# Running the combining product of an expert pair inside the next pair, in five PSUM banks

## What is computed

```python
for e in range(N_EXPERTS):
    gu = t @ w_gate_up[e] + b_gate_up[e]
    gate = jnp.minimum(gu[:, :D_EXPERT], SWIGLU_LIMIT)
    up = jnp.clip(gu[:, D_EXPERT:], -SWIGLU_LIMIT, SWIGLU_LIMIT)
    h = (up + 1.0) * (gate * jax.nn.sigmoid(SWIGLU_ALPHA * gate))
    out = out + comb[:, e:e + 1] * (h @ w_down[e] + b_down[e])
```

## Time and profile before

| | |
|---|---|
| median of three runs | 1267.7 us |
| the profiled execution | 1268.49 us |
| its span from first to last instruction | 1266.7 us (1.8 us lie around it) |
| TensorE busy | 1208.8 us, 95% |
| VectorE, ScalarE, GpSimd busy | 28%, 18%, 2% |
| moved by DMA | 446.69 MB, mean 353 GB/s |
| mean granted TensorE clock | 0.998 |

### The profile page before, as it was taken

How to read it: one execution, slowest core, us unless ns; L and a number is a source line. 1 busy time by engine, 2 the same in 40 slices (tenths; PEclk the granted TensorE clock), 3 DMA queues, 4 the chain that set the end, 5 groups by cost and what they waited for, 6 DMA issues and landing times.

```text
span 1266.7 us, 14158 instructions
## 1 busy us (share of the span) xinstructions
PE 1208.8 (95%) x5416; PEld 525.9 (42%) x5416; DVE 360.7 (28%) x826; ACT 225.2 (18%) x406; POOL 28.2 (2%) x62
## 2 busy tenths in 40 slices
PE   5999999999999999999999999999999999999997
PEld 3777777543333333333333333333333333333342
DVE  3564001253223132313233132323131321313233
ACT  2575110043101011101101010111011010101024
POOL 1001004000000000000000000000000000000000
PEclk9999999999999999999999999999999999999999
DMA  9725533437999999999999999999999999999931
GB/s 304 286 87 211 191 121 129 138 150 299 427 430 429 429 426 429 429 428 427 428 429 428 428 428 429 428 429 427 430 429 428 426 429 429 428 427 428 429 155 37
DMA packets 51027, 446.69 MB, mean 353 GB/s; under 512 B 8070, under 2 KB 9190, under 8 KB 26328
## 3 DMA queue, kind: packets, MB, share of 16 engines
q1 hardware_dynamic: 48304, 440.30, 83.5%
q0 software_dynamic: 2592, 6.10, 1.7%
q10 hardware_dynamic: 112, 0.03, 0.0%
HBM read 444.90 MB, written 1.88 MB: 353 GB/s over the span
## 4 chain that ended last, share of the span: by engine, by line
PE 74%; DMA 14%; DVE 6%; ACT 3%; issue 3%; ACTq 0%; POOL 0%; DVEq 0%; SPq 0%; POOLq 0%
PE ps L837 27%; PE ps L622 17%; PE ps L854 14%; DMA ring<-in_w_gate_up 12%; PE ps L905 6%; PE ps L811 3%; PE ps L935 2%; PE ps L823 2%; PE ps L614 1%; DVE work L1514 1%; DVE work L1507 1%; DVE work L1511 1%; ACT work L1134 1%; DMA work<-in_b_down 1%; ACT poolw L1144 1%
## 5 line engine op out<-in xcount | busy, mean ns | idle before, releaser
L837 PE MATMUL ps<-ring,work 128*64 128x512 f32 x2048 | 446.4, 592 | 5.1 <-DMA ring<-in_w_gate_up 5.1
L837 PEld LDWEIGHTS ps<-ring,work 128*64 128x64 f32 x2048 | 144.7, 137 | 288.5 <-issue 269.8
L854 PE MATMUL ps<-ring,gate_a 128*64 128x512 f32 x1024 | 225.9, 594 | 0.0
L622 PE MATMUL ps<-work,ring 128*128 128x288 f32 x768 | 191.4, 411 | 0.8 <-DVE work L1213 0.7
L622 PEld LDWEIGHTS ps<-work,ring 128*128 128x128 f32 x768 | 147.4, 192 | 42.1 <-issue 1.0
L854 PEld LDWEIGHTS ps<-ring,gate_a 128*64 128x64 f32 x1024 | 71.2, 137 | 133.2 <-issue 128.7
L1507 DVE TENSOR_SCALAR work<-ps 128x512 f32<-128x512 f32 x32 | 22.1, 692 | 354.8 <-PE ps L837 354.8
L1526 DVE TENSOR_TENSOR u_tok<-u_tok,ps 128x512 f32<-128x512 f32 (+1 forms) x96 | 65.7, 684 | 166.7 <-PE ps L905 166.2
L1134 ACT ACTIVATE work<-work 128x512 f32<-128x512 f32 x32 | 20.2, 630 | 489.2 <-DVE work L1507 489.2
L905 PE MATMUL ps<-poolw 128*128 128x512 f32 (+1 forms) x192 | 79.0, 611 | 23.3 <-ACT poolw L1144 23.1
L803 PE MATMUL ps<-x_tok,work 128*64 128x512 f32 x396 | 90.6, 592 | 0.0
(11 more groups left out here) (217 smaller groups left out, 652.1 us busy)
## 6 DMA issues: line engine op xcount, KB each, us to landing
ring<-in_w_gate_up SPq DMA_DIRECT2D x128, 2048.0 KB, 19.3
ring<-in_w_down SPq DMA_DIRECT2D x64, 2048.0 KB, 19.6
ring<-in_w_in SPq DMA_DIRECT2D x8, 2048.0 KB, 13.5
ring<-in_w_proj_b SPq DMA_DIRECT2D x2, 2048.0 KB, 7.8
ring<-in_w_proj_a SPq DMA_DIRECT2D x2, 2048.0 KB, 10.6
ring<-in_w_out SPq DMA_DIRECT2D x2, 2048.0 KB, 7.6
ring<-in_w_ple_gate SPq DMA_DIRECT2D x4, 1024.0 KB, 21.8
x_tok<-in_x_prompt SPq DMA_DIRECT2D x2, 512.0 KB, 3.9
```

Source lines behind the costliest of these rows:

```text
L622: mm = pe.matmul(out(b), lhs, rhs, start=(k == 0), stop=(k == len(pairs) - 1))
L837: mm = pe.matmul(ps[half(g), b, :], xg[:, k, :], whole_piece(q)[:, at + 512 * g:at + 512 * g + 512], start=False, stop=(k == KC - 1))
L854: mm = pe.matmul(ps[half(g), b, :], hT[:, 4 * j + i, :], whole_piece(q)[:, at + 512 * g:at + 512 * g + 512], start=False, stop=(4 * j + i ...
```

## The change

The product of a pair (the new add_pair on TensorE) is no longer issued at the end of its pair. It is issued in the next pair, behind the gate/up product of that pair's first expert and ahead of its gather. Its six results go to five banks (4, 5, 6, 7, 3): each of the first four has one of its own, and the two halves of the 32-token tile share bank 3, in which the transposes of sel_w also land. VectorE adds the six results behind the activation of the same expert. The first pair of the loop issues the product too; for that, VectorE zeroes o_pair (128 x 1024) and sel_wT (128 x 384) behind the normalised embedding, and TensorE waits for both ahead of its loop. After the loop one more product is issued for the last pair: 17 in all where there were 16. The waits of the tail follow the new count.

```diff
@@ -70,7 +70,7 @@
 
 
 CHUNK_BANK = {"gate": 0, "hT": 0, "xT": 1, "up": 1, "x": 2, "out": 2}
-B_S, B_Y = 3, [4, 5, 6]
+B_S, B_Y = 3, [4, 5, 6, 7, 3]
 PAIRS = NE // 2
 
 GATE_LOADS, SMALL_LOADS = 4, 3
@@ -336,6 +336,7 @@
         x_cleared = sem("x_cleared")
         x1_copied = sem("x1_copied")
         sel_w_ready = sem("sel_w_ready")
+        pair_cleared = sem("pair_cleared")
         x2_squared = sem("x2_squared")
         t_filled = [sem(f"tail_filled{b}") for b in range(8)]
         t_emptied = [sem(f"tail_emptied{b}") for b in range(8)]
@@ -403,9 +404,13 @@
             bank, turn = chunk_turn(kind, n)
             eng.wait_ge(emptied[bank], turn + (bank_uses[bank] + 1))
 
-        def pair_bank(i):
-
-            return B_Y[i % 3], i // 3
+        def pair_bank(t, h):
+
+            return B_Y[2 * t + h] if t < TT - 1 else B_Y[-1]
+
+        def sums_before(bank, m):
+
+            return (m * 2 if bank == B_S else m) + bank_uses[bank]
 
         tail_turns = plan_tail()
 
@@ -858,6 +863,18 @@
                         mm.then_inc(piece_used_up[q], 1)
                 mm.then_inc(filled[b], 1)
 
+            def add_pair(m):
+
+                chunk_read(pe, "out", m * 2 - 1)
+                for t in range(TT):
+                    for h in range(2):
+                        bank = pair_bank(t, h)
+                        pe.wait_ge(emptied[bank], sums_before(bank, m))
+                        mm = pe.matmul(ps[column_half(("y", t, h)), bank, :], sel_wT[:, t, 0:ROWS[t]],
+                                       o_pair[:, 512 * h:512 * h + 512], start=True, stop=True)
+                        if t < TT - 1 or h == 1:
+                            mm.then_inc(filled[bank], 1)
+
             embed(2, [0, 1])
             embed(1, [0])
             gather(0)
@@ -865,6 +882,7 @@
             chunk_read(pe, "x", 0)
             turn_rows("xT", 0, x_blocks)
             pe.wait_ge(bias_cast, BIAS_PARTS)
+            pe.wait_ge(pair_cleared, 2)
             pe.wait_ge(passes_ready, 1)
             passes = pe.value_load(passes_i[0:1, 0:1], min_val=1, max_val=PASSES)
             with pe.Fori(0, passes) as c:
@@ -878,6 +896,8 @@
                         chunk_read(pe, "xT", n)
                         weigh_gate_up(n)
 
+                        if i == 0:
+                            add_pair(m)
                         gather(n + 1)
                         pe.wait_ge(hidden_ready, n + 1)
                         turn_rows("hT", n, h_blocks)
@@ -885,7 +905,7 @@
                         turn_rows("xT", n + 1, x_blocks)
                         if i == 1:
                             pe.wait_ge(sel_w_ready, m + 1)
-                            pe.wait_ge(emptied[B_S], m + bank_uses[B_S])
+                            pe.wait_ge(emptied[B_S], m * 2 + (bank_uses[B_S] + 1))
                             for t in range(TT):
                                 mm = pe.transpose(ps[:, B_S, t * P:t * P + P], sel_w[:, t, :], ident[:])
                             mm.then_inc(filled[B_S], 1)
@@ -894,16 +914,7 @@
                         chunk_read(pe, "hT", n)
                         weigh_down(n)
 
-                    pe.wait_ge(emptied[B_S], m + (bank_uses[B_S] + 1))
-                    chunk_read(pe, "out", n)
-                    for t in range(TT):
-                        for h in range(2):
-                            bank, turn = pair_bank(2 * t + h)
-                            pe.wait_ge(emptied[bank], m * 2 + (bank_uses[bank] + turn))
-                        for h in range(2):
-                            bank, turn = pair_bank(2 * t + h)
-                            pe.matmul(ps[column_half(("y", t, h)), bank, :], sel_wT[:, t, 0:ROWS[t]],
-                                      o_pair[:, 512 * h:512 * h + 512], start=True, stop=True).then_inc(filled[bank], 1)
+            add_pair(passes * PAIRS)
 
 
             def begin_tail(name):
@@ -913,7 +924,7 @@
                 return bank
 
             for bank in B_Y:
-                pe.wait_ge(emptied[bank], passes * NE + bank_uses[bank])
+                pe.wait_ge(emptied[bank], sums_before(bank, passes * PAIRS) + 1)
             for t in range(TT):
                 for h in range(2):
                     b = begin_tail(("x2T", t, h))
@@ -1134,7 +1145,7 @@
                         nc.scalar.activation(sg, gate, ACT.Sigmoid, scale=ALPHA).then_inc(sig_ready, 1)
                         copy_inputs(n + 1)
                         if i == 1:
-                            act.wait_ge(filled[B_S], m + (bank_uses[B_S] + 1))
+                            act.wait_ge(filled[B_S], m * 2 + (bank_uses[B_S] + 2))
                             nc.scalar.copy(sel_wT.rearrange("p t s -> p (t s)"), ps[:, B_S, 0:TT * P]) \
                                 .then_inc(emptied[B_S], 1)
 
@@ -1145,10 +1156,9 @@
 
 
             for t in range(TT):
-                for i in range(2 * TT):
-                    if i // 2 == t:
-                        bank, turn = pair_bank(i)
-                        act.wait_ge(emptied[bank], passes * NE + (bank_uses[bank] + turn - 1))
+                for h in range(2):
+                    bank = pair_bank(t, h)
+                    act.wait_ge(emptied[bank], sums_before(bank, passes * PAIRS) + 1)
                 if t:
                     act.wait_ge(squares[3], t)
                 square_sums(3, t, x2[0:ROWS[t], t, :], square_tail)
@@ -1465,6 +1475,17 @@
                 b = chunk_filled(dve, "xT", n)
                 V.tensor_tensor(in_halves(xg), by_channel(b), in_halves(xg_gain), ALU.mult).then_inc(emptied[b], 1)
 
+            def add_pair(m):
+
+                for t in range(TT):
+                    for h in range(2):
+                        bank = pair_bank(t, h)
+                        dve.wait_ge(filled[bank], sums_before(bank, m) + 1)
+                        x_half = x2[0:ROWS[t], t, 512 * h:512 * h + 512]
+                        ins = V.tensor_tensor(x_half, x_half, ps[column_half(("y", t, h)), bank, :], ALU.add)
+                        if t < TT - 1 or h == 1:
+                            ins.then_inc(emptied[bank], 1)
+
             dve.wait_ge(gain_landed, 16)
             gathered(0)
 
@@ -1480,7 +1501,11 @@
                                                    op0=ALU.mult, op1=ALU.mult))
             step.need(last)
             dve.wait_ge(x1_copied, TT)
-
+            for t in range(TT):
+                for h in range(2):
+                    wait_filled(dve, ("ple", t, h))
+            V.memset(o_pair, 0.0).then_inc(pair_cleared, 1)
+            V.memset(sel_wT, 0.0).then_inc(pair_cleared, 1)
 
             dve.wait_ge(passes_ready, 1)
             passes = dve.value_load(passes_i[0:1, 0:1], min_val=1, max_val=PASSES)
@@ -1514,18 +1539,13 @@
                         V.scalar_tensor_tensor(out=up, in0=up, scalar=1.0, in1=gate, op0=ALU.add, op1=ALU.mult) \
                             .then_inc(hidden_ready, 1)
                         pick_expert(pick_gu, e + 1).then_inc(pick_gu_ready, 1)
+                        if i == 0:
+                            add_pair(m)
                         b = chunk_filled(dve, "hT", n)
                         V.tensor_copy(in_halves(hT), by_channel(b)).then_inc(emptied[b], 1)
                         gathered(n + 1)
 
-                    for i in range(2 * TT):
-                        bank, turn = pair_bank(i)
-                        dve.wait_ge(filled[bank], m * 2 + (bank_uses[bank] + turn + 1))
-                        t, at = i // 2, 512 * (i % 2)
-                        x_half = x2[0:ROWS[t], t, at:at + 512]
-                        V.tensor_tensor(x_half, x_half, ps[column_half(("y", t, i % 2)), bank, :], ALU.add) \
-                            .then_inc(emptied[bank], 1)
-
+            add_pair(passes * PAIRS)
 
             for t in range(TT):
                 for h in range(2):
```

## The result

The changed kernel takes 1286.01 us (median of four runs, 1285.51 to 1286.96) against 1267.74 us: a ratio of 1.0139, 95% interval 1.0127 to 1.0151, 18.3 us slower. The forecast was 1285.9 us. The profiled execution takes 1285.67 us (span 1283.8), 17.2 us above the profiled execution of before.

A forecast was written before the change was run, and what follows sets the result against it. The prediction took the weight stream at 429 GB/s as the bound. Its terms, 12.0 + 3.1 + 3.0 + 0.1 = 18.2 us, gave 1286.7 us for the profiled execution and a median of 1285.9 us, range 1280.7 to 1290.2.

The forecast's parts named there:

- The bound: Expert stage: the weight stream at 429 GB/s sets the end; TensorE time saved in a pair is worth nothing.
- TensorE's own pair: TensorE's time for a pair, falling by 1.44 + 0.5 to some 55.8 us; credited 0 beside the transfers.
- later start: Ahead of the loop: TensorE waits for VectorE's zeroing, so gate/up starts near 301.0 instead of 289.02; 12.0 us (10.5 to 13).
- slow stretch: First products after TensorE's 12 us standstill run slower, as at the kernel's start; 3.1 us (0 to 6).
- hole: First pair, the gap: its extra sum delays the fifth piece's issue, so the stream runs dry once; 3.0 us (2.3 to 4.2).
- end: Behind expert 31's last gate/up piece: TensorE 0.6 us late, final sum saves 0.45; together +0.1 us (-0.9 to +1.3).
- the opening: Start of the trace: 16 products take 0.440 each against 0.249 later, 3.1 us lost; source of the slow stretch.
- VectorE's 1.57 us of idle time: VectorE's idle ahead of 298.63, used to gauge TensorE's restart after the zeroing; 1.4 us taken (0 to 1.6).
- the fifth piece of expert 3: Second pair: effective 83.7 us after the gate/up start, with the queue busy until 86.8, so no further gap.
- A: Rival: the weight stream is not the bound and mirrors TensorE's demand; -11.5 us, 1256 us; chance 0.04.
- B: Rival: the late start is absorbed, leaving only gap and end; 1270.8 us, or 1267.7 with stream slack; chance 0.03.
- C: Rival: the stream runs dry in further pairs, at experts 3 and 5; +2 to 6 us, 1288 to 1292; chance 0.13.

The follow-up runs named there:

- e2: The changed kernel without the sum of zeros in the first pair, hence without the zeroing and its wait: 1269.17 us, ratio 1.0006.
- e3: The kernel before the change with its pair sums left out (product and adds), so the experts' share of the output is missing: 1262.03 us, ratio 0.9949.
- e4: The kernel before the change with only the two zeroings and TensorE's wait for them ahead of the loop added: 1282.93 us, ratio 1.0114.
- e8: e2 with the sum moved ahead of the last quarter of the gate/up product of the pair's first expert: 1298.8 us, ratio 1.0243.

## Why the prediction held

**The bound** held: a steady rate, waits that replace the ones removed, pairs at 58.7 us. e2 shows it by a faster TensorE, e3 by a much faster one. TensorE's own pair was put at 55.8 us and measured 55.85; the chain first runs through a transfer in the fifth pair, where the third or fourth had been named.

**The terms**, by the two profiled executions:

| term | forecast | measured | how |
|---|---|---|---|
| later start | 12.0 | 12.0 | transposes to gate/up start: 300.72 - 286.94 = 13.78, before 1.74 |
| front of the kernel | - | -0.3 | the transposes themselves: 286.94 for 287.28 |
| slow stretch | 3.1 | 1.6 | gate/up start to first request: 5.40 for 3.81 |
| hole | 3.0 | 3.3 | windows 326 to 332 |
| end | +0.1 | +0.4 | landing of expert 30's fourth piece to the tail: 52.84; before 23.12 + 29.36 = 52.48 |
| sum | 18.2 | 17.0 | tail's transposes: 1237.56 - 1220.54 = 17.0 |

The one mis-sized term is the slow stretch; with the 0.4 us that the slow bias products lost, counted in the first row, the slow clock cost 2.0. The forecast had the first request of expert 1 near 308 to 309 us, and it came at 306.1, mostly for this reason. The row it came from, the opening, is no fixed cost: the same 16 products took 5.80 us in the changed kernel's trace and 7.04 before. In three executions the stretch ahead of the first request cost 1.6, 1.9 and 2.5 us. The terms make 17.0 us while the medians stand 18.3 apart, and 17.5 apart in the later comparison. The profiled executions stand 0.8 above and 0.3 below their medians, which accounts for the first difference; it is not a further mechanism that any run shows. So it is luck that the forecast hits the median to 0.1 us: its terms are 1.2 us too long together, and those two distances make up for it. What the runs bear out is the mechanism, each term to within 1.5 us.

The step by which the late start was made of queue waits, zeroing and a register load came out to 0.3 us, though it put the zeroing's end at 299.1 and TensorE's restart 1.4 us later. They were 298.3 and 1.6, and the bias products took 0.85 us for 0.5: errors that cancel in part. VectorE's 1.57 us of idle time, taken as the measure of such a restart, did not come again on VectorE itself: its loop follows the second zeroing at once (298.31). Some of the sums are off by a little: the steps to the zeroing's end add up to 299.0, the gap to 2.9 us, and the fifth piece of expert 3 to 83.9 us, which changes nothing in the argument. The sum in its new place was put at 4.4 us and takes 4.61, part of why the hole is 3.3 us.

**The rivals.** A fell with e3. B would have needed the zeroing to be covered; e4 alone costs 14.5 us. C, further holes, did not come: after 353 us no slice of the expert stage is below 426. A close relative of it did in e8, where TensorE's pair passed that of the transfers.

## What to carry to other kernels

When a stream of transfers runs without a pause, ask only three things of a change: does the stream start later, does it run dry, and what is behind its last byte; time saved in between comes back as waits. A wait that makes a loop safe belongs at the first instruction that needs it, not ahead of the loop (14 us here). And work moved between two instructions of a queue takes its cover from what runs beside it there, so moving either one must be costed on both engines.

## What the runs showed that was not expected

In e8 the granted clock fell behind a wait of only 2.87 us of TensorE, from 1.00 to between 0.53 and 0.62 in the windows shown; TensorE had been busy 1.43 of the 4 us from 362 to 366. It did so in ten of 15 pairs and cost 1.7 to 2.7 us of the down product each time; behind the same wait in the other five pairs it cost nothing (7.09 us), and no run shows what decides between the two. I had counted on such a loss only after the 12 us pause.

The granted clock of the opening reads 1.00 while single records of its products last up to 821 ns, twice the 406 of later ones; at 300 us the same column shows 0.50 and 0.52 for such a stretch. The durations were the better guide there, since the loss after the pause was real; whether it is the clock that slows the opening, and why the column doesn't show it, stays open.
